# A hybrid encoder block on one core: the mixer in two calls, half of the tokens retrieved between them, and the rows of one sparse tile gathered earlier

## The chip, the cores and the metric

The kernel runs on one core of one Trainium2 chip. The metric is the device time of one execution in microseconds (us); the time of the kernel before is the median of three runs. The trace comes from one further execution that was profiled; its span (first to last instruction) and its own device time stand side by side in the table below.

## The reference

One layer on x of 1024 tokens x 1024 features, all float32:

```
proj = x @ w_in
A    = gated DeltaNet(4 heads x 128: causal conv of 4 on q, k, v; chunked delta rule; gated RMS norm)
B    = sliding-window attention(8 query heads x 64, 2 kv heads, window 128, learned sinks)
x1   = LayerNorm(alpha * x + concat(A, B) @ w_out)
per head of 8 (product keys): q1, q2 = halves of x1 @ wq;  s1 = q1 @ keys1^T, s2 = q2 @ keys2^T   (128 keys each)
       top 16 of s1, top 16 of s2, top 16 of their 256 sums -> ids = 128 * key1 + key2, gate = softmax
ffn  = sum over the 128 picks of a token: gate * gelu(x1 . u[id]) * v[id]      (16384 experts, u and v of 1024 features)
out  = LayerNorm(alpha * x1 + ffn)
```

The recurrence of A runs over the tokens in order. What token t retrieves needs x1 of token t alone.

## The kernel before

All sizes are in tiles of 128 tokens (`NT` = 8). The function `build` (L2042) calls the stages one after the other; `stage_semaphores` ends each with a barrier of all engines, so that no stage overlaps the next.

`project` (L118) computes the projections and writes them to DRAM. It is not touched.

`mix_tokens` (L365) runs over the eight tiles in order. Inside a tile the triangular solve is a chain of seven levels (`LV` = 6 and a last one): PE multiplies (L629, L632), DVE masks (L919), adds (L926, L934) and hands back to PE. Between the steps of the chain DVE does pieces of the next tile (`ahead`, L830), and PE does pieces of the output projection of the tile before (`project_out`, L520). After the levels DVE updates the recurrent state (L957), normalizes the two halves of the mix (L963 to L977), and finishes the layer norm of the tile before (`layer_norm` L882, `normalize` L897). POOL applies scale and shift to that row block `h1`, and SP stores it (L494), which also paces SP's loads of x (L461). In the first tile DVE splits the eight 512 KB pieces of `w_out` into a high and a low part (`split_wout`, L904), and PE has no output projection there. SP's loads are L458, L461 and L483.

`split_x1` (L1005) loads x1 (L1023), transposes it and splits it into high and low parts for PE.

`retrieve` (L1049) does the eight heads for all eight token tiles at once: queries on PE, scores, then the selection on DVE (L1279 is its first operation of a head, L1339 its last, L1353 a part of the tail), the turning of positions into keys on POOL and ACT. On PE it also computes the first 12 of the blocks of `hidden` (matmul of u against x1 for the dense tokens) that a later stage would otherwise do.

`index_picks` (L1420) computes the row numbers `id_u`, `id_v` and transposes the picks of the dense tiles.

From here the tokens are in two halves. Tiles 0 to 3 (`NS` = 4) are **sparse**: for each of a tile's 128 picks, POOL gathers 128 rows of u (one for each token, 128x1024, one indirect DMA of 512 KB), and DVE takes the dot product with x1 (one instruction and a read of its accumulator; rings of `U_RING` = 4 buffers). For v, POOL gathers 128 rows by token (`V_RING` = 6 buffers), and PE sums them with weights: a **V step** is four gathered blocks and 8 matmuls of 128x32 by 128x512 (`weigh_rows`, L1804), 32 steps a tile. Tiles 4 to 7 are **dense**: all 16384 experts are computed for them with a gate that is zero where an expert was not picked.

`build_gates` (L1468) makes that gate for the dense tiles: 32 steps of 16 tokens. In each, DVE builds one-hot rows `g_two` (L1549, 16 instructions) and `g_one` (L1555, 16), PE multiplies them (L1511, 16 matmuls), ACT copies the result, and SP stores 4 MB after every fourth step (`s_G<-g_tile`). Beside it POOL gathers the U rows of sparse tile 0 (L1566), DVE dots them (L1540, four a step), and PE computes 8 more hidden blocks (L1523 to L1525, six matmuls of 128x512 in each step), with DVE splitting u (L1533).

`experts` (L1617) runs over 64 groups of 256 experts. A group loads its u, v and gate (L1706 is the gate), computes hidden (L1778 to L1780, left out for the first `SHORT` = 10 groups, whose hidden blocks exist by then), the gating, and the values (L1799 to L1801), which DVE adds up (L1946). Beside this run the sparse tiles: `PHASE` says at which groups tile s begins. Between two of them DVE takes the dots of tile s+1 (L1742 gathers, L1955 dots; 128 rows spread over the phase's length less one group) and PE weighs the V rows of tile s (L1751 gathers, L1813 matmuls). The last lines norm and store the output.

What sets the order is each engine's program text, with counted semaphores between engines, and the two tables that `spread` (L1607) makes from `PHASE`:

```
PHASE = (0, 18, 36, 54, 64)
for s in range(NS - 1):   spread(PHASE[s], PHASE[s + 1] - 1.0, P, U_SLOTS)        # U rows of tile s + 1
for s in range(NS):       spread(PHASE[s] + 0.5, PHASE[s + 1] - 0.1, 32, V_SLOTS) # V steps of tile s
```

## Time and profile before

| what | value |
|---|---|
| device time, median of 3 runs | 3643.05 us |
| lowest and highest | 3635.28 and 3651.44 us |
| the profiled execution, its own device time | 3627.19 us |
| its span | 3625.5 us |
| mean granted clock of TensorE | 0.893 of full |
| busy: PE / DVE / ACT / POOL | 2872.9 / 2381.2 / 931.5 / 1537.2 us |
| DMA over the span | 829.68 MB, mean 229 GB/s |

The stages, by the first instruction of each: project 0 to 302.66, mixer to 791.79, split to 812.86, retrieval to 1234.20, numbering to 1242.66, gates to 1675.16, experts to the end; the third phase's end (group 54) lies at 3222.38. A stage's length counts in full, since a barrier stands between two of them. A busy time is the time in which an engine executed something; a share of DMA is the mean busy share of the 16 DMA engines.

### The profile page before, as it was taken

To read this page: it belongs to the slowest core of one execution; us is meant where nothing else is said; L and a number is where in the kernel's file an instruction comes from. 1 tells how busy PE (TensorE), PEld (TensorE's weight loads), DVE (VectorE), ACT (ScalarE), POOL (GpSimd) and SP (SyncE) were. 2 spreads that over 40 slices of the span, in tenths; PEclk is the share of its full clock that TensorE was granted. 3 is DMA by queue.
4 is the path that set the end of the run, shared out by engine and by line. 5 is a ranking of instruction groups with operands and counts; after the bars stand their busy time and mean duration, and the time that the engine had idled before them with its cause. 6 is when DMAs were issued, how large, how long until landed. Compare 5 with 4: busy or idle time off the path is not lost.

```text
span 3625.5 us, 40035 instructions
## 1 busy us (share of the span) xinstructions
PE 2872.9 (79%) x14408; PEld 2219.2 (61%) x14408; DVE 2381.2 (66%) x5368; ACT 931.5 (26%) x1295; POOL 1537.2 (42%) x1196
## 2 busy tenths in 40 slices
PE   7996899969776355553667989999998998898886
PEld 6896788857665254452344666666676666665554
DVE  4403666645999899994667767777676766653335
ACT  4312222223333233331111222222222222222111
POOL 0000011113776543334565655666655565633333
PEclk9987999989888677776788999999999999999998
DMA  4312121112110377777999999999999999977774
GB/s 136 116 47 83 59 61 61 42 65 74 44 44 25 107 253 240 272 263 282 345 368 370 375 344 334 377 340 367 353 332 354 351 358 350 345 264 263 265 260 166
DMA packets 367789, 829.68 MB, mean 229 GB/s; under 512 B 158048, under 2 KB 180704, under 8 KB 366592
## 3 DMA queue, kind: packets, MB, share of 16 engines
q0 software_dynamic: 150864, 548.60, 41.1%
q1 hardware_dynamic: 216752, 278.84, 23.2%
q8 instruction: 100, 1.64, 0.2%
q14 instruction: 73, 0.60, 0.0%
HBM read 768.49 MB, written 58.85 MB: 228 GB/s over the span
## 4 chain that ended last, share of the span: by engine, by line
DMA 23%; PE 12%; DVE 9%; POOL 6%; issue 3%; ACT 1%; SPq 0%; POOLq 0%; DVEq 0%; ACTq 0%
DMA e_vr<-in_v 10%; DMA hold<-in_v,id_v 6%; DMA e_u_row<-in_u,id_u 5%; POOL hold L1751 4%; PE psum L1813 4%; DVE e_u_row L1955 3%; DVE e_y L1946 2%; PE psum L1799 2%; PE psum L1800 2%; PE psum L1801 1%; POOL e_u_row L1742 1%; DMA e_g<-s_G 1%; PE psum L1778 1%; DVE e_vl L1917 1%; PE psum L1780 1%
## 5 line engine op out<-in xcount | busy, mean ns | idle before, releaser
L1751 POOL DMA_INDIRECT hold<-in_v,id_v x512 | 565.0, 1104 | 421.1 <-PE psum L1813 285.2
L1742 POOL DMA_INDIRECT e_u_row<-in_u,id_u x384 | 467.1, 1217 | 473.4 <-DVE hidden_s L1955 376.1
L1955 DVE CUSTOM_DVE_ANT_0 e_u_row<-e_u_row,hold 128x1024 f32<-128x1024 f32 x384 | 466.9, 1222 | 101.9 <-DMA e_u_row<-in_u,id_u 101.7
L1799 PE MATMUL psum<-e_vh,e_ah 128*128 128x512 f32 x1024 | 432.0, 422 | 112.7 <-DVE e_y L1946 104.5
L1800 PE MATMUL psum<-e_vl,e_ah 128*128 128x512 f32 x1024 | 418.9, 409 | 0.0
L1946 DVE TENSOR_TENSOR e_y<-e_y,psum 128x512 f32<-128x512 f32 x504 | 328.5, 680 | 134.1 <-PE psum L1801 133.9
L1801 PE MATMUL psum<-e_vh,e_al 128*128 128x512 f32 x1024 | 415.8, 406 | 0.0
L1813 PE MATMUL psum<-hold,e_column 128*32 128x512 f32 x2048 | 276.3, 661 | 170.5 <-DMA hold<-in_v,id_v 170.5
L1799 PEld LDWEIGHTS psum<-e_vh,e_ah 128*128 128x128 f32 x1024 | 204.3, 200 | 237.9 <-DVE e_y L1946 121.2
L1778 PE MATMUL psum<-x1d_hi,e_uh 128*128 128x512 f32 x864 | 343.1, 397 | 0.0
L1511 PE MATMUL psum<-g_one,g_two 128*128 128x128 f32 x1024 | 187.9, 368 | 191.3 <-issue 175.5
L1779 PE MATMUL psum<-x1d_lo,e_uh 128*128 128x512 f32 x864 | 337.4, 390 | 0.0
L1780 PE MATMUL psum<-x1d_hi,e_ul 128*128 128x512 f32 x864 | 336.5, 389 | 0.0
L1511 PEld LDWEIGHTS psum<-g_one,g_two 128*128 128x128 f32 x1024 | 182.7, 281 | 204.2 <-issue 204.2
L1929 DVE TENSOR_TENSOR e_a<-e_a,e_g 128x512 f32<-128x512 f32 x108 | 74.5, 690 | 311.8 <-ACT e_a L1858 157.9
L1566 POOL DMA_INDIRECT hold<-in_u,id_u x128 | 166.4, 1300 | 248.3 <-DVE hidden_s L1540 219.4
L1813 PEld LDWEIGHTS psum<-hold,e_column 128*32 128x32 f32 x2048 | 61.1, 116 | 307.1 <-issue 301.6
L1858 ACT ACTIVATE e_a<-psum 128x512 f32<-128x512 f32 x108 | 64.1, 593 | 678.9 <-PE psum L1780 678.9
L1801 PEld LDWEIGHTS psum<-e_vh,e_al 128*128 128x128 f32 x1024 | 203.9, 199 | 46.5
L1917 DVE TENSOR_TENSOR e_vl<-e_vr,e_vh 128x1024 fp32r<-128x1024 f32 x128 | 156.2, 1220 | 112.5 <-ACT e_vh L1847 112.5
L1800 PEld LDWEIGHTS psum<-e_vl,e_ah 128*128 128x128 f32 x1024 | 204.8, 200 | 40.9
L1847 ACT ACTIVATE e_vh<-e_vr 128x1024 fp32r<-128x1024 f32 x128 | 135.3, 1057 | 358.7 <-DMA e_vr<-in_v 352.3
(313 smaller groups left out, 5639.3 us busy)
## 6 DMA issues: line engine op xcount, KB each, us to landing
e_vr<-in_v SPq DMA_DIRECT2D x128, 512.0 KB, 6.6
e_ur<-in_uT SPq DMA_DIRECT2D x108, 512.0 KB, 6.9
s_G<-g_tile SPq DMA_DIRECT2D x8, 4096.0 KB, 13.8
e_g<-s_G SPq DMA_DIRECT2D x128, 256.0 KB, 13.1
p_wr<-in_w_ch SPq DMA_DIRECT2D x17, 512.0 KB, 3.8
s_ch<-p_out POOLq DMA_DIRECT2D x16, 512.0 KB, 3.8
m_ch<-s_ch SPq DMA_DIRECT2D x8, 1024.0 KB, 5.9
r_w<-in_wq SPq DMA_DIRECT2D x16, 512.0 KB, 4.1
```

What stands on the lines that cost most here:

```text
L1511: last = nc.tensor.matmul(psum[:, n // 4, (n % 4) * NK:(n % 4 + 1) * NK], one2[s][:, n, :], one1[s][:, n, :], start=True, stop=True)
L1742: pool.indirect_dma_start(out=u_ring[n % U_RING][:], out_offset=None, in_=io["u"], in_offset=bass.IndirectOffsetOnAxis(ap=id_u[:, s, k:k + ...
L1751: pool.indirect_dma_start(out=v_ring[m % V_RING], out_offset=None, in_=io["v"], in_offset=bass.IndirectOffsetOnAxis(ap=id_v[:, t:t + 1], a ...
L1778: nc.tensor.matmul(psum[:, j, :], uh[j][:, k, :], x1d[0][:, k, :], start=(k == 0), stop=False)
L1779: nc.tensor.matmul(psum[:, j, :], uh[j][:, k, :], x1d[1][:, k, :], start=False, stop=False)
L1780: last = nc.tensor.matmul(psum[:, j, :], ul[j][:, k, :], x1d[0][:, k, :], start=False, stop=(k == KC - 1))
L1799: nc.tensor.matmul(acc, ah[s][j][:, r], vh[s][j][:, c], start=(j == 0), stop=False)
L1800: nc.tensor.matmul(acc, ah[s][j][:, r], vl[s][j][:, c], start=False, stop=False)
L1801: last = nc.tensor.matmul(acc, al[s][j][:, r], vh[s][j][:, c], start=False, stop=(j == 1))
L1813: last = nc.tensor.matmul(psum[32 * j:32 * j + 32, 6 + c, :], column[:, n % Z_RING, j, 31 - i:63 - i], v_ring[(4 * n + j) % V_RING][:, c * ...
L1946: add = nc.vector.tensor_tensor(y[:, t, c], y[:, t, c], psum[:, 2 + q % 4, :], ALU.add)
L1955: nc.vector.tensor_tensor_reduce(row, row, xs[:, s, :], 1.0, 0.0, ALU.mult, ALU.add, hs[:, s, k:k + 1]).then_inc(dotted, 1)
```

## The change

The mixer is called twice, for tiles 0 to 3 and for tiles 4 to 7; the state and the small per-tile factors live outside it, its loops are written out, the input `xt` and `mixT` have one buffer instead of two, and the scores' buffer `sc` half its size. Each call loads and splits `w_out`. Between the calls `split_x1`, `retrieve` and a new `number_rows` (the part of `index_picks` that computes `id_u`, `id_v`, `gate_s`) run for the 512 sparse tokens. After the second call `split_x1`, `retrieve` and a new `turn_picks` (the other part) run for the 512 dense tokens. The second retrieval computes 16 hidden blocks, two a head, all of them split on DVE or ACT and none on POOL; the first computes none. No hidden block is left in `build_gates`, so that 16 are ready for `experts` instead of 20.

The second mixer call gathers the 128 U rows of sparse tile 0 on POOL and takes the dots on DVE; two of its four ring buffers are the landing buffers of `w_out`, so the first gather waits for the last split. `build_gates` gathers the V rows of sparse tile 0 and weighs them, one V step after each step's one-hot matmuls, and builds `g_one` with one instruction a step. `experts` has sparse tiles 1 to 3 left for V and begins with the U rows of tile 1.

The core of the diff:

```diff
-TAIL = 4
-AHEAD_R = PH + TAIL
-AHEAD_G = TD // TG
+AHEAD = 2 * PH
-PHASE = (0, 18, 36, 54, 64)
-AHEAD = AHEAD_R + AHEAD_G
+PHASE = (0, 11, 32, 53, 64)
...
+            ring = [sb(f"m_row{n}", [P, D]) for n in range(U_RING)]
+            wout_raw = ring[:2]
...
+                def dot_rows(count):
+
+                    if dots:
+                        for k in islice(row_numbers, count):
+                            if k == 0:
+                                dve.wait_ge(x0_in, 16)
+                            dve.wait_ge(row_in[k % U_RING], 16 * (k // U_RING + 1))
+                            row = ring[k % U_RING][:]
+                            nc.vector.tensor_tensor_reduce(row, row, x0[:], 1.0, 0.0, ALU.mult, ALU.add,
+                                                           hs[:, 0, k:k + 1]).then_inc(dotted, 1)
...
                         if n < LV - 1:
+                            if before:
+                                dot_rows(2)
                             dve.wait_ge(lt, c * (LV - 1) + n + 1)
                             nc.vector.tensor_tensor(tu[:, 0], tu[:, 0], bank(2), ALU.add).then_inc(la, 1)
...
                         if not before and n:
                             split_wout(n - 1)
+                        if before:
+                            dot_rows(1)
...
                     if after:
                         begin_inverse(c + 1)
+                    if before:
+                        dot_rows(4)
...
                     if not before:
                         for k in range(LV, KC):
                             split_wout(k)
+                        dot_rows(20)
+                    dot_rows(4)
...
                     last.then_inc(S["og"], 1)
+                    dot_rows(4)
...
                     if before:
                         normalize(c - 1)
+                    dot_rows(4)
...
+                def gather_rows(c):
+                    for k in range(c * P // N, (c + 1) * P // N):
+                        if k >= U_RING:
+                            pool.wait_ge(dotted, k - U_RING + 1)
+                        else:
+                            pool.wait_ge(wout_lo, KC)
+                        pool.indirect_dma_start(out=ring[k % U_RING][:], out_offset=None, in_=io["u"],
...
+                for c in range(N):
+                    if dots:
+                        gather_rows(c)
+                    if c:
+                        scale_shift(c - 1)
+                scale_shift(N - 1)
...
+def number_rows(nc, sem, cst, psum, key1, key2, gate, id_u, id_v, gate_s):
+                nc.vector.scalar_tensor_tensor(idf[:], key1[:], float(NK), key2[:], ALU.mult, ALU.add).then_inc(numbered, 1)
...
+def turn_picks(nc, sem, scr, cst, psum, key1, key2, gate, xs, pickT):
...
+                def weigh_rows(n):
...
-                        nc.tensor.matmul(out, uh[:, k, :], x1d[0][:, k, :], start=(k == 0), stop=False)
-                        nc.tensor.matmul(out, uh[:, k, :], x1d[1][:, k, :], start=False, stop=False)
-                        last = nc.tensor.matmul(out, ul[:, k, :], x1d[0][:, k, :], start=False, stop=(k == KC - 1))
+                    weigh_rows(q)
...
-                    for n in range(R):
-                        t = q * R + n
-                        last = nc.vector.tensor_scalar(one1[s][:, n, :], iota, pickT[:, 0, t:t + 1], None, ALU.is_equal)
-                    last.then_inc(hot1[s], 1)
-                    if q % PER == 0:
-                        split_u(q // PER)
-                    dot_rows(U_STEP * q + U_STEP // 2, U_STEP * (q + 1))
+                    nc.vector.tensor_tensor(one1[s][:], iota.unsqueeze(1).broadcast_to([P, R, NK]),
+                                            pickT[:, 0, q * R:(q + 1) * R].unsqueeze(2).broadcast_to([P, R, NK]),
+                                            ALU.is_equal).then_inc(hot1[s], 1)
...
-        for s in range(NS):
+        for s in range(1, NS):
             for at, ns in spread(PHASE[s] + 0.5, PHASE[s + 1] - 0.1, 32, V_SLOTS).items():
-                steps[at] = [32 * s + n for n in ns]
+                steps[at] = [32 * (s - 1) + n for n in ns]
```

**DVE in the levels of the mixer.** A tile's levels on DVE, before: m_tu is the solve's buffer, m_xs the masked product, m_dm, m_qd and m_aq belong to the next tile.

```order
L917 REGISTER_ALU
L919 TENSOR_TENSOR m_xs<-psum,cst 128x512
L846 ISA
L847 TENSOR_TENSOR m_qd<-m_ch,m_eg 128x512
L925 REGISTER_ALU
L926 TENSOR_TENSOR m_tu<-m_tu,psum 128x512
L934 TENSOR_TENSOR m_tu<-m_tu,psum 128x512
L851 TENSOR_TENSOR m_aq<-psum,m_dm 128x512
L917 REGISTER_ALU
L919 TENSOR_TENSOR m_xs<-psum,cst 128x512
L925 REGISTER_ALU
```

The same place in the second call after the change (L926 is now the dot and the read of its accumulator, L948 and L956 are the former L926 and L934; a name that ends in _4 is a buffer of the second call):

```order
L939 TENSOR_TENSOR m_xs<-psum,cst 128x512
L926 ISA m_row_4,hidden_s<-m_row_4,m_x_4 128x1024
L926 ISA hidden_s 128x1
L926 ISA m_row_4,hidden_s<-m_row_4,m_x_4 128x1024
L926 ISA hidden_s 128x1
L948 TENSOR_TENSOR m_tu<-m_tu,psum 128x512
L956 TENSOR_TENSOR m_tu<-m_tu,psum 128x512
L852 TENSOR_TENSOR m_dm<-psum,m_e_4 128x512
L926 ISA m_row_4,hidden_s<-m_row_4,m_x_4 128x1024
L926 ISA hidden_s 128x1
L939 TENSOR_TENSOR m_xs<-psum,cst 128x512
L855 TENSOR_TENSOR m_qd_4<-m_ch_4,m_eg 128x512
```

Three dots of 128x1024 have come into each level, two of them ahead of the addition for which PE waits.

**POOL in the second mixer call.** After the change (m_h is the row block h1 of the layer norm, m_row the ring):

```order
L1033 DMA m_row_4<-in_u,id_u 128x1024 x64
L1039 TENSOR_TENSOR m_h_4<-m_h_4,m_lng 128x1024
L1041 TENSOR_TENSOR m_h_4<-m_h_4,m_lnb 128x1024
L1033 DMA m_row_4<-in_u,id_u 128x1024 x32
L1039 TENSOR_TENSOR m_h_4<-m_h_4,m_lng 128x1024
L1041 TENSOR_TENSOR m_h_4<-m_h_4,m_lnb 128x1024
```

64 gathers stand ahead of the first scale and shift, and 32 ahead of each of the next two. Before, POOL had only the pairs of scale and shift in this stage.

**PE in the gate building.** Two steps before:

```order
L1511 MATMUL psum<-g_one,g_two 128x128 x16
L1523 MATMUL psum<-x1d_hi,g_uh 128x512
L1524 MATMUL psum<-x1d_lo,g_uh 128x512
L1525 MATMUL psum<-x1d_hi,g_ul 128x512
L1523 MATMUL psum<-x1d_hi,g_uh 128x512
L1524 MATMUL psum<-x1d_lo,g_uh 128x512
L1525 MATMUL psum<-x1d_hi,g_ul 128x512
L1511 MATMUL psum<-g_one,g_two 128x128 x16
```

And its beginning after the change (L1537 turns the activated dots of tile 0, L1545 is the former L1511):

```order
L1537 MATMUL psum<-cst,hidden_s 128x128
L1545 MATMUL psum<-g_one,g_two 128x128 x16
L1530 MATMUL psum<-hold,g_column 32x512 x8
L1545 MATMUL psum<-g_one,g_two 128x128 x16
L1530 MATMUL psum<-hold,g_column 32x512 x8
```

Six matmuls of 128x512 a step have left, and eight of a gathered block against a 32-column weight have come.

## Rows read from the trace of the kernel before

**Rows 1.** Windows: length, busy us of PE, PEld, DVE, ACT, POOL; PEclk, DMA, GB/s

```profile
302.66:791.79 489.13, 417.47 (x2756) 365.78 (x2756) 280.79 (x504) 123.42 (x268) 37.78 (x16) 0.92 0.18 56
791.79:812.86 21.07, 10.06 (x64) 8.41 (x64) 9.80 (x8) 8.20 (x8) 0.00 (x0) 0.81 0.50 199
812.86:1234.20 421.34, 293.07 (x1312) 240.72 (x1312) 367.50 (x1639) 151.13 (x129) 261.10 (x109) 0.84 0.13 46
...
1242.66:1675.16 432.50, 232.47 (x1216) 213.90 (x1216) 389.22 (x1288) 144.16 (x144) 166.38 (x128) 0.75 0.71 248
1675.16:3222.38 1547.22, 1323.65 (x6170) 938.56 (x6171) 1071.50 (x1618) 336.27 (x505) 908.15 (x774) 0.92 0.97 353
3222.38:3590.00 367.62, 307.45 (x1502) 201.93 (x1501) 135.55 (x176) 71.32 (x116) 124.05 (x123) 0.95 0.74 248
```

**Rows 2.** Windows, same columns: four tiles in the middle of the mixer

```profile
455.00:665.00 210.00, 199.04 (x1376) 174.29 (x1375) 133.32 (x240) 54.63 (x125) 18.12 (x9) 0.98 0.17 52
```

**Rows 3.** Timeline of SP in the mixer: start, us, engine, line, transfer [idle before]

```profile
302.66 0.33 SPq L474 DMA_DIRECT2D m_sinks<-in_sinks  x1
...
458.47 0.37 SPq L494 DMA_DIRECT2D s_x<-m_h  x1
...
511.57 0.36 SPq L494 DMA_DIRECT2D s_x<-m_h  x1
...
721.29 0.35 SPq L494 DMA_DIRECT2D s_x<-m_h  x1
...
768.93 18.60 SPq L494 DMA_DIRECT2D s_x<-m_h  x2
791.79 3.75 SPq L1023 DMA_DIRECT2D t_x<-s_x  x8
```

**Rows 4.** Timeline of DVE: the first operation behind the mixer's preparation

```profile
314.82 0.69 DVE L835 COPY m_gB<-m_rows 128x1024 f32<-128x1024 f32 x1
```

**Rows 5.** Waits of DVE, 455 to 665: total us, times, longest

```profile
DVE m_tu L926 <- PE psum L629: 46.9, 20, 3.6
...
DVE m_on L977 <- PE psum L668: 4.8, 4, 1.9
```

**Rows 6.** Timeline of DVE in the gates: the first dot

```profile
1248.90 1.23 DVE L1540 CUSTOM_DVE_ANT_0 hold<-hold 128x1024 f32<-128x1024 f32 x1 [1.82 <-DMA hold<-in_u,id_u]
```

**Rows 7.** Timeline of POOL in the gates: the first and the fifth gather

```profile
1243.44 1.02 POOL L1566 DMA_INDIRECT hold<-in_u,id_u  x1 [10.49 <-POOLq L115]
...
1250.40 1.83 POOL L1566 DMA_INDIRECT hold<-in_u,id_u  x1 [2.13 <-DVE hidden_s L1540]
```

**Rows 8.** U gathers of the gates, L1566, all 128

```profile
DMA to landing us min/median/max: 4.2/5.2/15.2
```

**Rows 9.** The same line while a 4 MB store is under way, 1349 to 1364

```profile
DMA to landing us min/median/max: 10.9/12.9/14.3
```

**Rows 10.** DVE's last operation of a head, L1339: ns min/median/max, first to last start

```profile
L1339 DVE TENSOR_TENSOR gate<-r_ex,r_gsum x8: 291/3252/3257, 894.2 to 1213.1; 128x128 f32<-128x128 f32 x8
```

**Rows 11.** Lines of DVE in the gates: busy us, mean ns | idle before

```profile
L1549 DVE TENSOR_SCALAR g_two<-cst,hold 128x128 f32<-128x128 f32 x512 | 134.2, 348 | 5.9 <-PEq L115 5.9
```

**Rows 12.** A comparison of 128x2048 on DVE, L1353

```profile
L1353 DVE TENSOR_TENSOR hold<-r_pf,cst x1: 2276/2276/2276, 1216.3 to 1216.3; 128x2048 f32<-128x2048 f32 x1
```

**Rows 13.** Page, costliest groups, the gates' U gathers: busy, mean ns | idle before

```profile
L1566 POOL DMA_INDIRECT hold<-in_u,id_u x128 | 166.4, 1300 | 248.3 <-DVE hidden_s L1540 219.4
```

**Rows 14.** U gathers of the experts, L1742, all 384

```profile
DMA to landing us min/median/max: 4.3/8.2/10.6
```

**Rows 15.** Timeline of PE in the last phase: two V steps

```profile
3244.61 1.92 PE L1813 MATMUL psum<-hold,e_column 128*32 128x512 f32 x16
...
3253.64 1.92 PE L1813 MATMUL psum<-hold,e_column 128*32 128x512 f32 x16 [1.42 <-DMA hold<-in_v,id_v]
```

**Rows 16.** V gathers of the last phase, L1751, 3240 to 3590: count, then landing

```profile
L1751 POOL DMA_INDIRECT hold<-in_v,id_v x122: 932/941/1980, 3246.8 to 3573.4; - x122
...
DMA to landing us min/median/max: 4.1/6.0/10.9
```

More of the change, by code:

```diff
@@ L1015, in part @@
         def part(t, which):
-            x1, first = (x1s, 0) if t < NS else (x1d, NS)
-            return x1[which][:, :, (t - first) * P:(t - first + 1) * P]
+            return x1[which][:, :, t * P:(t + 1) * P]
         with nc.Block() as block:
@@ L1036, in _ @@
             def _(act):
-                for t in range(NT):
+                for t in range(NT // 2):
                     act.wait_ge(tr[t % 2], t // 2 + 1)
@@ L1042, in _ @@
             def _(dve):
-                for t in range(NT):
+                for t in range(NT // 2):
                     dve.wait_ge(hi[t % 2], t // 2 + 1)
@@ L1117, in store_hidden @@
                     sp.dma_start(scr["hidden"][b], act_out[b % 2][:]).then_inc(h_out[b % 2], 16)
-                def head(h):
+                for h in range(PH):
                     for s in range(2):
@@ L1477, in build_gates @@
         PER = TG // R
-        U_STEP = P // STEPS
-        xs = hold[:, 0:NS, :]
-        ring = [hold[:, 6 + n, :] for n in range(U_RING)]
+        x0 = hold[:, 0, :]
+        ring = [hold[:, NS + n, :] for n in range(V_RING)]
         one1 = [sb(f"g_one{s}", [P, R, NK]) for s in range(2)]
@@ L2086, in build @@
[L2086 to L2087 removed]
+        with ExitStack() as mixer:
+            small = {n: sb(mixer, f"m_{n}", [P, NT, GH])
+                     for n in ("lnbeta", "g", "gam", "nkey", "kdl", "kdec", "nbeg", "decay", "beta")}
+            rows = sb(mixer, "m_rows", [P, NT, 2, GH])
+            state = sb(mixer, "m_state", [P, GH, P])
+            with stage_semaphores(nc) as sem:
+                mix_tokens(nc, sem, io, scr, ba, cst, psum, small, rows, state, 0)
+            with ExitStack() as sparse:
+                x1s = [sb(sparse, f"x1s_{n}", [P, KC, TS], F32R) for n in ("hi", "lo")]
+                key1, key2, gate = picks(sparse, "early")
+                with stage_semaphores(nc) as sem:
+                    split_x1(nc, sem, scr, cst, psum, x1s, 0)
+                with stage_semaphores(nc) as sem:
+                    retrieve(nc, sem, io, scr, cst, psum, x1s, key1, key2, gate, False)
+                with stage_semaphores(nc) as sem:
+                    number_rows(nc, sem, cst, psum, key1, key2, gate, id_u, id_v, gate_s)
+            with stage_semaphores(nc, "_late") as sem:
+                mix_tokens(nc, sem, io, scr, ba, cst, psum, small, rows, state, NS, dots=(id_u, hs))
```

781 lines of the change are left out of this document (382 added, 399 removed).

## The prediction

> **What bounds the kernel now.** I read the windows by stage first, because a barrier stands between stages and each one's length counts in full. In [rows 1] the reader sees six different limits. The mixer (489.13 us) has PE busy for 417 us and DVE for 281: it is a chain that passes between the two, and in its middle PE is busy 199.04 of 210 us [rows 2]. The retrieval (421.34 us) has DVE busy for 367.5. The gates (432.50 us) have DVE busy for 389.22, and the experts' first 54 groups (1547.22 us, 28.65 a group) have DMA at 0.97 with 353 GB/s and PE busy for 1323.65, 24.5 a group. The last ten groups (367.62 us, 36.8 a group) have DMA at 0.74, PE at 307 and DVE at 136. Nothing is full there, and the timeline of PE shows why: V steps start at 3244.61 and 3253.64, 9.0 us apart, the second after a wait for gathered rows [rows 15]. 122 gathers from 3246.8 to 3573.4 are 10.7 us for four [rows 16], so 32 steps take 32 x 10.7 = 342 us of that phase. The change takes work from the two DMA- and DVE-bound stages and gives it to the mixer, where DVE shows 8 idle microseconds in 20. The question is whether those are free.
>
> **The mixer in two calls: +62.** The stores of the row blocks date the tiles [rows 3]: the first block is stored 155.8 after the stage's start, the next 53.1 later, the last but one 47.6 after the one before it, the last 18.3 later (they are the pair of 18.60), and 4.6 after it the next stage begins. A call of four tiles is 155.8 + 53.1 + 47.6 + 18.3 + 4.6 = 279.4. The second call has no preparation of the small factors; DVE's first tile work starts 12.2 after the stage's start [rows 4], of which some 4.7 for the loads stays, so 7.5 go. 2 x 279.4 - 7.5 - 489.1 = +62. The repeated w_out split is inside the 155.8.
>
> **The 128 dots: +139.** A dot takes 1.23 us on DVE [rows 6]. In the first late tile 24 stand in a row behind the last split, and a ring of four feeds them. The first gather starts only then: in the gates the first gather started at 1243.44 and the first dot at 1248.90, 5.5 later [rows 6, 7]. A buffer's cycle is the issue's gap 0.3, 5.2 to landing [rows 8], 1.23 for the dot and a little for the hand-over, 7.0 in all, so 1.75 a row: 24 x 1.75 = 42. Eight more at about 1.5 are 12, of which DVE's wait for PE at L977 (1.2 a tile [rows 5]) covers 1.9 with its neighbours. Nothing else of the chain can pass DVE meanwhile. Sum 5.5 + 42 + 12 - 2 = 58. In each of the other three tiles 32 dots are 39.2 us. Two in each of five levels stand where DVE waited for PE anyway, 46.9 us in four tiles, and the 4.8 at L977 also [rows 5]: 12.9 a tile are covered. The rest, 26.3, is on the chain, and with one short wait for a ring emptied while POOL does a scale and shift (18.12 us for nine operations [rows 2], two a tile) it is 27, in three tiles 81. 58 + 81 = +139. PE's fill work hides behind this, not the other way round. Bounds: 104 dots' excess entirely covered, +58; nothing covered and each at the ring's pace, at 1.83 + 0.3 a row [rows 7], 128 x 2.13 + 5.5 = +278.
>
> **Retrieval +53, split and numbering +12.5.** L1339 ends DVE's work of a head: 894.2 to 1213.1 for eight, 45.6 a head [rows 10]. The first head ended 81.3 after the start [rows 1, 10], so 36 went before DVE's first selection, and 21 after the last. With half the tokens a head costs 23.3 (half of the selection, small operations whole). Call one, without hidden blocks: 24 to start, 8 x 23.3, 11 of tail = 222. Call two has two splits of u a head, 2.4 us of DVE, and loads twice as many: 32 + 8 x 26.1 + 11 = 252. Together 474 against 421.3. The loads of x1 and the barriers come twice: +7 for the split, +5.5 for the numbering (8.46 before).
>
> **The gates: -42.** DVE falls far below the stage: g_two costs 134.2 for 32 steps [rows 11], and one comparison of 128x2048 took 2.28 us [rows 12], so 4.2 + 2.3 = 6.5 a step. What ends last is the V chain. Its step is 9.0 in [rows 15] and 10.7 as a mean of the phase [rows 16]. To the 9.0 to 9.4 that two steps there show I add 0.8 for slower issue beside DVE's comparisons (1300 ns [rows 13] against a median of 941 [rows 16], twice in a chain) and 0.5 for a lower clock, since PEclk is 0.75 here [rows 1]: 10.6, times 32 = 339. Seven stores of 4 MB meet the gathers; while one is under way landing takes 12.9 instead of 5.2 [rows 8, 9]. Not all of 7.7 shows, I take 6.3: 44. With 7 to start the stage is 390 against 432.5. Bounds: no gain (0), and 32 x 9.0 + 12 = 300 (-132).
>
> Here a row and a rule differ in size. POOL's gather took 1.83 us right behind a dot, 1.02 at the start of the stage [rows 7], and 1300 ns is the mean of all. The Trainium skill (SBUF — State Buffer, "SBUF: two separate sides") says that GpSimd cannot write the descriptors of its transfers while a VectorE instruction of certain kinds holds the port pair that they share. By that rule every gather beside DVE would take the 1.83: two on a V step's chain make 1.8 us instead of 0.8, 32 more for the gates, and a row of the burst takes 2.13 instead of 1.75, 9 more. The sum would be +145 instead of +104.5. I take the measured mean of 1300 ns, in which both kinds are mixed; the rule's size lies within my range.
>
> **The experts: -120.** 128 gathers of V rows leave, 67 MB. Groups 0 to 10: U rows of tile 1 are 12.8 a group instead of 7.5, no V rows, no hidden in the first eight. DVE was busy 19.8 a group [rows 1]; 5.3 dots at 1.3 more make 26.7. The ring of four gives one row in (8.2 + 1.23 + 0.3) / 4 = 2.4 us at the experts' landing time [rows 14], less when V gathers don't compete: 31 a group at most. I take 29.5: 325 for eleven. Groups 11 to 52, 42 of them: 6.4 U rows and 1.5 V steps a group are 9.0 MB, which at 353 GB/s [rows 1] is 25.5, close to PE's 24.0 to 24.5. I take 26.3: 1105. The last eleven groups hold the same 32 steps and no U rows, 32 x 10.7 plus the lead-in: the same 368 [rows 1, 16]. The tail of 35.5 stays. 325 + 1105 + 368 + 35.5 = 1833 against 1950, and with four more hidden loads and matmuls less an early start of the V steps I round to -120. Bounds: -75 (27.3 a group) and -178 (PE alone at 24.5, short groups at 28).
>
> **Sum.** 62 + 139 + 53 + 12.5 - 42 - 120 = +104.5. On the span of 3625.5 this is 3730, on the profiled execution's own 3627.19 about 3732. The median shown, 3643.05, lies 16 above that execution, so the median is 3732 + 16 = 3748; I say **3747 us**.
>
> **Rivals.**
> 1. *TensorE's clock falls in the places that DVE now holds up* (chance 0.14). The mixer's granted clock is 0.98 where PE is busy 95% [rows 2], and 0.75 in the gates, where it is busy 54% [rows 1]. A late tile of 80 us with 50 of PE work would, at the lower level (1.2 GHz instead of 2.4), need up to 100: 3 x 20 = 60, and a V step's 1.92 [rows 15] would become 3.84, part of 32 x 1.9. About +85: 3830. Against it: hidden blocks and fill remain. The Trainium skill (TensorE: Matmul & The Clock Gate, "HAM oscillation") holds that an engine which keeps waiting between bursts is throttled again; by it this rival would be the rule.
> 2. *The costs come as worked out, but the chains relax* (0.10): the gates at 341 (-92, V steps of 9.4 and stores hidden) and the experts at -172. Net +2.5: 3646, no change.
> 3. *The experts turn out DMA-bound throughout, and lose what DMA loses* (0.10), the other side. 65 MB at 353 GB/s [rows 1] are 184 us; if groups 11 to 52 take 24.7, the first eleven 25, and the last phase's V steps run at 9.4, near the 9.0 of [rows 15], for 32 x 1.3 = 42 less, the stage is 1676, -274, net -50: 3593. It decides once the experts save more than 224 us, that is all other terms together. Against it: PE's 24.5 a group leaves no room, and the last phase was slow with DMA at 0.74 already.
>
> **How the numbers follow.** The forecast, 3700 to 3790, has 0.66. The range takes in the second rival and half of the first: 3640 to 3830. 0.5% (18 us) is about what a measurement of this kernel can tell from no change. Faster: rival 3 and a bit of rival 2, 0.11. Same: the rest of rival 2, 0.09. Slower: the forecast and rival 1, 0.80.
>
> **What would show it.** The first late tile should hold a block of 24 dots on DVE of 45 to 50 us with PE idle, its tiles 1 to 3 should take near 80 us between stores, and DVE's wait at the level's first addition should have gone. The two calls of the mixer should sum to about 690, the retrievals to 474, the gates should be near 390 with PE's V matmuls waiting for POOL's rows and DVE under 60% busy, groups 11 to 52 near 26 us with DMA still over 0.95. It is wrong if the mixer calls sum to under 620 (the dots hid), if the gates are over 430 or under 330, or if PEclk in the second mixer call is under 0.85.

## The result and the profile after

| | before | after |
|---|---|---|
| device time, median | 3642.5 us (4 runs) | 3766.57 us (4 runs) |
| lowest to highest | 3635.28 to 3651.44 | 3760.72 to 3789.43 |
| ratio, 95% interval | | 1.035 (1.030 to 1.040) |
| profiled execution, own time and span | 3627.19, 3625.5 | 3760.72, 3759.1 |
| TensorE's granted clock | 0.893 | 0.875 |
| busy PE / DVE / ACT / POOL | 2872.9 / 2381.2 / 931.5 / 1537.2 | 2868.1 / 2388.5 / 951.4 / 1576.6 |

The change costs 3.5%, with the forecast of 3747 us 20 us below the median and inside the range. The busy time of each engine moved by under 3%. What changed is where the work stands, and what waits for it there. The windows by stage of the kernel after (window, length, busy us of PE, PEld, DVE, ACT, POOL, then PEclk, DMA share, GB/s) answer to [rows 1]:

```profile
301.55:574.63 273.08, 214.81 (x1380) 188.11 (x1380) 146.57 (x264) 68.01 (x144) 18.84 (x8) 0.87 0.20 60
574.63:588.35 13.72, 5.81 (x32) 5.00 (x32) 4.90 (x4) 4.10 (x4) 0.00 (x0) 0.72 0.41 153
588.35:809.60 221.25, 118.49 (x512) 98.13 (x512) 182.42 (x862) 70.12 (x89) 150.43 (x106) 0.75 0.14 43
...
812.86:1043.82 230.96, 118.07 (x688) 103.55 (x688) 152.97 (x251) 37.68 (x72) 82.74 (x66) 0.70 0.62 202
1043.82:1129.17 85.35, 55.41 (x344) 47.53 (x344) 74.44 (x127) 13.86 (x31) 46.64 (x34) 0.82 0.65 211
1129.17:1209.39 80.22, 48.31 (x296) 40.48 (x296) 68.50 (x116) 10.55 (x27) 44.07 (x34) 0.82 0.69 223
1209.39:1239.56 30.17, 13.41 (x48) 10.43 (x48) 7.07 (x13) 0.29 (x1) 4.68 (x2) 0.73 0.15 52
1239.56:1253.92 14.36, 5.80 (x32) 4.99 (x32) 4.90 (x4) 4.10 (x4) 0.00 (x0) 0.71 0.40 147
1253.92:1515.22 261.30, 201.58 (x896) 165.52 (x896) 197.57 (x878) 114.20 (x134) 158.89 (x106) 0.89 0.26 85
1515.22:1524.30 9.08, 3.00 (x12) 2.15 (x12) 0.36 (x1) 2.60 (x5) 0.00 (x0) 0.50 0.61 231
1524.30:1914.49 390.19, 233.56 (x1537) 146.54 (x1537) 206.57 (x548) 121.25 (x163) 129.91 (x128) 0.78 0.71 259
1914.49:2250.27 335.78, 176.04 (x609) 137.24 (x610) 258.52 (x410) 51.74 (x63) 167.08 (x138) 0.74 0.89 300
2250.27:3351.51 1101.24, 1062.45 (x5049) 784.38 (x5049) 808.22 (x1194) 280.83 (x408) 609.30 (x508) 0.99 0.95 342
3351.51:3723.60 372.09, 326.03 (x1598) 219.77 (x1597) 148.38 (x192) 77.15 (x124) 124.20 (x123) 0.96 0.75 252
3723.60:3759.10 35.50, 12.29 (x47) 9.02 (x45) 28.36 (x41) 7.68 (x10) 20.64 (x8) 0.69 0.30 118
```

In order: first mixer call, split, retrieval of the sparse half (the numbering of 3.3 us is left out), the second mixer call in four pieces that end at its stores and its last barrier, split, retrieval of the dense half, turning of the picks, gates, experts in groups 0 to 10, 11 to 52, 53 to 63, and the tail. As a balance of the spans:

| stage | before | forecast of the difference | measured after | difference |
|---|---|---|---|---|
| mixer, 1 or 2 calls | 489.1 | +201 | 273.1 + 426.7 | +210.7 |
| split of x1 | 21.1 | +7 | 13.7 + 14.4 | +7.0 |
| retrieval | 421.3 | +53 | 221.3 + 261.3 | +61.3 |
| numbering, turning | 8.5 | +5.5 | 3.3 + 9.1 | +3.9 |
| gates | 432.5 | -42 | 390.2 | -42.3 |
| experts and tail | 1950.3 | -120 | 1844.6 | -105.7 |
| projection | 302.7 | 0 | 301.6 | -1.1 |
| span | 3625.5 | +104.5 | 3759.1 | +133.6 |

The spans differ by 133.6 us and the medians by 124, since the profiled execution of the kernel before lies 15 us below its median and that of the kernel after 6. A stage also differs from one execution to the next: the experts' code of the kernel after, from their first load to the end, took 1844.6, 1862.8, 1829.3, 1867.5, 1864.8 and 1865.0 us in the profiled executions of that kernel and of runs 1 to 5 below. Fifteen us more or less in that stage are therefore no finding.

The loss is in the second mixer call. The waits of DVE (total us, times, longest), over that whole call:

```profile
DVE m_row L926 <- DMA m_row<-in_u,id_u: 43.5, 43, 5.6
DVE m_h L895 <- PE psum L527: 13.6, 1, 13.6
DVE m_tu L948 <- PE psum L630: 13.3, 10, 4.3
DVE m_sc L874 <- PE psum L533: 9.2, 4, 2.7
```

DVE waits 43.5 us for gathered rows, where [rows 5] have no such wait; 25.7 us of it lie in the first late tile, up to 962. Its wait for PE at the level's first addition (now L948) is 13.3 us. The page's rows of what POOL and DVE do there and in the gates answer to [rows 13] and [rows 11]:

```profile
L1033 POOL DMA_INDIRECT m_row<-in_u,id_u x128 | 156.6, 1224 | 226.6 <-DVE hidden_s L926 122.8
L1580 POOL DMA_INDIRECT hold<-in_v,id_v x128 | 129.9, 1015 | 255.4 <-PE psum L1530 215.9
L1562 DVE TENSOR_SCALAR g_two<-cst,pickT 128x128 f32<-128x128 f32 x512 | 134.4, 351 | 156.2 <-PE psum L1545 156.2
...
L1530 PE MATMUL psum<-hold,g_column 128*32 128x512 f32 x512 | 103.6, 952 | 142.0 <-DMA hold<-in_v,id_v 142.0
```

The gates' DVE now waits 156 us for PE, and the gates' V matmuls wait 142 us for rows: the bound of that stage moved from DVE to the chain of gather, landing and V step.

### The profile page after: what moved, and what is told of

Same layout as the page of the kernel before. It is cut to its first block, busy times and chain, and to the rows that moved or that the text cites. A ratio compares the mean times of both kernels' runs of the same rounds, so it can differ in the third digit from the quotient of the medians.

```text
span 3759.1 us, 39825 instructions
## 1 busy us (share of the span) xinstructions
PE 2868.1 (76%) x14408; PEld 2200.5 (59%) x14408; DVE 2388.5 (64%) x4994; ACT 951.4 (25%) x1389; POOL 1576.6 (42%) x1299
## 4 chain that ended last, share of the span: by engine, by line
PE 23%; DMA 14%; DVE 8%; issue 2%; POOL 2%; ACT 1%; POOLq 0%; SPq 0%; DVEq 0%; ACTq 0%
DMA e_vr<-in_v 5%; DMA hold<-in_v,id_v 4%; PE psum L1827 4%; DMA e_u_row<-in_u,id_u 4%; PE psum L1813 4%; PE psum L1814 3%; PE psum L1815 3%; PE psum L1792 3%; PE psum L1793 3%; PE psum L1794 3%; DVE e_u_row L1969 3%; DVE e_y L1960 2%; DMA e_g<-s_G 1%; DVE e_vl L1931 1%; POOL hold L1765 1%
## 5 line engine op out<-in xcount | busy, mean ns | idle before, releaser
L1792 PE MATMUL psum<-x1d_hi,e_uh 128*128 128x512 f32 x896 | 355.4, 397 | 0.0
L1793 PE MATMUL psum<-x1d_lo,e_uh 128*128 128x512 f32 x896 | 350.4, 391 | 0.0
L1794 PE MATMUL psum<-x1d_hi,e_ul 128*128 128x512 f32 x896 | 349.3, 390 | 0.0
L1033 POOL DMA_INDIRECT m_row<-in_u,id_u x128 | 156.6, 1224 | 226.6 <-DVE hidden_s L926 122.8
L1562 DVE TENSOR_SCALAR g_two<-cst,pickT 128x128 f32<-128x128 f32 x512 | 134.4, 351 | 156.2 <-PE psum L1545 156.2
L1827 PE MATMUL psum<-hold,e_column 128*32 128x512 f32 x1536 | 192.2, 619 | 48.2 <-DMA hold<-in_v,id_v 48.0
L1530 PE MATMUL psum<-hold,g_column 128*32 128x512 f32 x512 | 103.6, 952 | 142.0 <-DMA hold<-in_v,id_v 142.0
L1792 PEld LDWEIGHTS psum<-x1d_hi,e_uh 128*128 128x128 f32 x896 | 168.5, 188 | 73.3 <-issue 38.5
```

The lines of the kernel that those rows point to most:

```text
L1033: pool.indirect_dma_start(out=ring[k % U_RING][:], out_offset=None, in_=io["u"], in_offset=bass.IndirectOffsetOnAxis(ap=id_u[:, 0, k:k + 1 ...
L1792: nc.tensor.matmul(psum[:, j, :], uh[j][:, k, :], x1d[0][:, k, :], start=(k == 0), stop=False)
L1793: nc.tensor.matmul(psum[:, j, :], uh[j][:, k, :], x1d[1][:, k, :], start=False, stop=False)
L1794: last = nc.tensor.matmul(psum[:, j, :], ul[j][:, k, :], x1d[0][:, k, :], start=False, stop=(k == KC - 1))
L1827: last = nc.tensor.matmul(psum[32 * j:32 * j + 32, 6 + c, :], column[:, n % Z_RING, j, 31 - i:63 - i], v_ring[(4 * n + j) % V_RING][:, c * ...
```

## The experiments

Every run below was compared with the kernel before on the same chip; "before" is the median there. These medians lie between 3632.62 and 3639.84 us, that of the result at 3642.5, so a difference of 10 us between a run and the kernel after is not told apart. Spans are of the profiled execution.

**1. The dots left out.**

```diff
-                row_numbers = iter(range(P))
+                row_numbers = iter(())
...
-                    if dots:
-                        gather_rows(c)
```

> The changed kernel with its second mixer call stripped of the 128 gathers and dots of sparse tile 0 (left out of the computation: hidden_s of tile 0 is set to zero). Theory (the dots sit on DVE's side of the chain): the second call falls from 426.7 us to that of the first call less its preparation, 273 - 7.5 = 266, so the kernel loses some 160 us, 3767 -> about 3607; gates and experts stay within 5 us. Rival (the second call is long because w_out is loaded again and its tiles start cold, the dots are mostly covered): the call stays above 340 us and the kernel above 3680.

Measured: 3608.49 us against 3635.19 before, ratio 0.991 (0.988 to 0.995). The second call, from its first load at 818.00 to the next stage's at 1081.66, took 263.7 us; the theory said 266. Windows of that call here and, below, of the kernel after:

```profile
818.00:1081.66 263.66, 214.00 (x1376) 187.20 (x1376) 143.99 (x249) 62.35 (x131) 18.88 (x8) 0.89 0.21 64
```

```profile
812.86:1239.56 426.70, 235.21 (x1376) 201.98 (x1376) 302.98 (x504) 62.38 (x131) 178.13 (x136) 0.75 0.61 197
```

DVE's busy time differs by 159.0 us, the call's length by 163.0. The dots are paid in full; what they fill of DVE's idle time comes back as waits for rows. Here the same view of waits as above, without dots:

```profile
DVE m_tu L949 <- PE psum L630: 44.9, 20, 4.3
...
DVE m_rms L997 <- ACT m_rms L773: 5.7, 3, 1.9
DVE m_sc L875 <- PE psum L533: 3.9, 4, 1.1
DVE m_on L1007 <- PE psum L669: 3.5, 4, 1.0
```

At the level's first addition (L949 here) 44.9 became 13.3, so 31.6 us were indeed covered, and at L997 and L1007 some more; and 43.5 us of waits for rows took their place. The wait for PE at L875 (L874 in the kernel after) grew, from 3.9 to 9.2 us; "The clock" below returns to it. This run also shows that the rest of the change, without the price of the dots, is 27 us faster than the kernel before. The two calls of the mixer by themselves cost 273.1 + 263.7 - 489.1 = 47.7 us.

**2. The first late tile's 32 dots left out.**

```diff
-                        dot_rows(20)
-                    dot_rows(4)
+                    if before:
+                        dot_rows(4)
...
-                    if dots:
-                        gather_rows(c)
+                    if dots and c:
+                        gather_rows(c - 1)
```

> The changed kernel without the 32 dots of the first late tile (96 rows gathered and dotted, all in the three tiles behind it, at the same places; the last 32 rows are left out of the computation). Theory (24 dots in a row, fed by a ring of four, stop the chain, and 8 more): the call is shorter by 58 to 75 us, the kernel near 3700. Rival (PE has work to do meanwhile, and the price is in the levels of tiles 1 to 3): under 30 us.

Measured: 3704.41 us, 62 below the kernel after. The second call took 363.4 us, 63.3 less. That is near the 58 of the forecast, but the stores of the row blocks date it better. The first one comes 163.9 us after the call's start here and 231.0 in the kernel after, so the first tile's dots cost 67 us. The stretches behind it are alike (84.3 and 79.6 us between stores, against 85.4 and 80.2), up to the last store; from there to the next stage it is 9.3 us here, in which no engine works, and 4.1 in the kernel after and in run 1. What brings these 5 us was not tried. Without them the other 96 dots cost 363.4 - 263.7 - 5.1 = 94.6 us, 31.5 a tile where the forecast had 27.

**3. All dots in the three later tiles.**

```diff
                         if before:
-                            dot_rows(1)
+                            dot_rows(2)
...
-                    for k in range(c * P // N, (c + 1) * P // N):
+                    for k in range(c * P // 3, (c + 1) * P // 3):
...
-                    if dots:
-                        gather_rows(c)
+                    if dots and c:
+                        gather_rows(c - 1)
```

> The changed kernel with the same 128 dots, but none in the first late tile and 43, 43 and 42 in the three behind it (two instead of one at each level's end, 6, 6, 5 and 4 outside the levels). Theory (what counts is the number of dots on the chain at 1.23 us each, and the burst also pays 1.75 us a row for its ring and 5.5 for its start): 11 more dots in each of three tiles cost 13.5 us each, 40, against 58 to 75 saved: the kernel is 20 to 35 us faster than the changed one, about 3740. Rival (the ring of four cannot feed 43 rows a tile): as slow as the changed kernel or slower, with waits for rows inside the levels.

Measured: 3776.58 us, 10 above the kernel after: the theory's 20 to 35 us of gain did not come. The second call took 429.4 us against 426.7. Two tiles of it (1010 to 1218) have this view of waits on DVE:

```profile
DVE m_row L926 <- DMA m_row<-in_u,id_u: 33.6, 26, 6.0
DVE m_sc L874 <- PE psum L533: 5.5, 2, 2.7
```

These are 33.6 us of waits for rows in two tiles, up to 6.0 each, where the kernel after has 11.0 in the same two. The rival was right that the rows are what is short, but this run has a cause of its own beside the ring. The first two tiles gather 42 and 43 rows and take 43 dots each, so the last dot of either tile needs a row whose gather stands behind the scale and shift of the tile before. It waits 5.9 us in the first (to 1011.37) and 6.0 in the second (to 1121.30). These 11.9 us could hide more than half of a gain of 20. Without them the call would be some 9 us shorter than in the kernel after, still short of the theory; the rest are shorter waits, up to 5.0 us, at dots that follow one another closely, as the ring of four gives them. I had treated the ring's pace as a matter of the burst alone.

**4. Only the dots ahead of a level's first addition.**

```diff
-                row_numbers = iter(range(P))
+                row_numbers = iter(range(30))
...
-                        if before:
-                            dot_rows(1)
```

> The changed kernel with only the 30 dots that stand ahead of the first addition of a level (two in each of five levels of the three later tiles of the second call); the other 98 rows are left out of the computation. Without any dot DVE waited there for PE, 22.4 us in two tiles, and the second call took 263.7 us. Theory (dots in a place where DVE waits are free up to the length of that wait): 12.3 us of dots a tile against 11.2 of wait, the call stays under 275 us and the kernel near 3615. Rival (a dot costs its 1.23 us wherever it stands, since its row or PE's next work comes later too): 30 x 1.25 = 37 more, the call about 301 us, the kernel 3646.

Measured: 3623.97 us against 3632.62. The call took 280.6 us, between the two: 17 above the call without dots, not 37. DVE's waits in two of its tiles:

```profile
DVE m_row L927 <- DMA m_row<-in_u,id_u: 12.0, 2, 6.6
DVE m_tu L949 <- PE psum L630: 4.9, 6, 1.4
```

These two, 12.0 us, are the only waits for a row in the whole call; the first of the three tiles has none. From the call's start to its first store, which holds that tile's ten dots, the call takes 142.7 us against 141.7 in run 1: ten dots, 12.3 us of work, cost 1.1. The next two tiles take 8.3 and 9.0 us more than in run 1, of which 5.4 and 6.6 are the waits for a row. So 12.0 of the 17 us are late rows, and some 5 are dots that were longer than their gap; over the call DVE is busy 34.2 us more, and its wait at L949 fell from 44.9 to 17.9. POOL's timeline of this run says where the row was:

```profile
956.89 2.36 POOL L1032 TENSOR_TENSOR m_h<-m_h,m_lng 128x1024 f32<-128x1024 f32 x1 [30.68 <-DVE m_h L909]
959.33 2.37 POOL L1034 TENSOR_TENSOR m_h<-m_h,m_lnb 128x1024 f32<-128x1024 f32 x1
961.84 0.98 POOL L1026 DMA_INDIRECT m_row<-in_u,id_u  x1
```

The first gather of the tile was issued at 961.84, behind the scale and shift of the tile before, and the dot that wanted it waited 5.40 us until 968.57. So a dot in a gap is nearly free, and here the first row of a tile is not, because of its place in POOL's queue. In the kernel after this particular wait does not occur: there a tile's last four dots stand behind the normalization, and the next tile's first dots come 12 us after its first gather (1056.12 and 1043.94) and wait for nothing.

**5. Nine buffers for the V rows of the gates.**

```diff
-        ring = [hold[:, NS + n, :] for n in range(V_RING)]
+        GR = 9
+        ring = [hold[:, NS + n, :] if n < V_RING else sb(f"g_row{n}", [P, D])[:] for n in range(GR)]
```

> The changed kernel with nine buffers instead of six for the V rows of the gate building (the experts keep six). Theory (the stage is a chain of gathers, landing and one V step, 11.8 us a step with PE waiting 142 us for rows): with a whole step's rows ahead the chain opens, and the stage goes from 390 us towards the bound of its bytes, 101 MB at 353 GB/s = 285, say 310: the kernel about 3690. Rival (ACT's evacuation or PE at the low clock bounds the step): the stage stays over 370.

Measured: 3683.55 us, 83 below the kernel after. The window of the stage:

```profile
1523.67:1819.00 295.33, 200.10 (x1537) 138.64 (x1537) 205.10 (x548) 123.84 (x163) 157.54 (x128) 0.83 0.91 342
```

295 us instead of 390, with DMA at 0.91 instead of 0.71. It is the chain that bound the stage. Opened, it stands near the 285 estimated from its bytes; that the bytes are the next bound was not tried. PE's wait for rows fell from 142.0 to 76.4 us. The stage is 95 us shorter and the medians 83 apart; the experts' 1865.0 us of this execution, against 1844.6, are of the size by which that stage differs anyway.

**6. One part of the change alone: `g_one` in one comparison.** (On the kernel before.)

```diff
-                    for n in range(R):
-                        t = q * R + n
-                        last = nc.vector.tensor_scalar(one1[s][:, n, :], iota, pickT[:, 0, t:t + 1], None, ALU.is_equal)
+                    nc.vector.tensor_tensor(one1[s][:], iota.unsqueeze(1).broadcast_to([P, R, NK]), ...
```

> The kernel before with one part of the change alone: g_one of a step in one comparison of 128x2048 (2.28 us) instead of sixteen (3.22). Theory (the gate building before is bound by DVE, 389 busy of 432): DVE loses 103.0 - 73 = 30 us and the stage the same, the kernel -30, 3635 -> about 3605. Rival (the U rows' ring or the gathers beside a comparison that reads two tensors hold it up): no gain, DVE's waits for rows grow from 25 by what the comparison saves.

Measured: 3615.51 us against 3639.84, ratio 0.994 (0.991 to 0.997). The stage is some 21 us shorter (busy DVE 389 to 358), and DVE's waits for rows grew from 25.3 to 34.3 us: the theory, less a third of the rival.

**7. Ten V buffers in the last phase.** (On the kernel before. The four U buffers are idle there.)

```diff
+        def v_slot(m):
+            return m % V_RING if m < LAST else (m - LAST) % (V_RING + U_RING)
```

> The kernel before with ten buffers instead of six for the V rows of the last phase alone (the four of the U rows are idle then). Theory (the last phase is bound by the chain of gather, landing and V step, 10.7 us a step): the phase goes from 367.6 us to PE's 307 with gaps, about 315, the kernel -50. Rival (the bound is the values' chain with DVE and the loads of u and v): within 10 us of the kernel before.

Measured: 3567.45 us against 3639.84, ratio 0.979 (0.974 to 0.984), more than expected. The last ten groups of this run:

```profile
3243.00:3537.00 294.00, 291.64 (x1501) 196.01 (x1500) 135.19 (x175) 71.40 (x116) 125.63 (x123) 1.00 0.88 310
```

294.0 us instead of 367.6, with PE busy for 291.6 of it at the full clock: the phase passed from a chain of latencies to PE. PE's busy time shrank by 16 us too, from 307.5 to 291.6, with its granted clock at 1.00 instead of 0.95 (307.5 x 0.95 = 292). That is why the gain passed the estimate, which had PE at 307.

**8. Runs 6 and 7 together**

> Both of the last two edits on the kernel before. They touch different stages with a barrier between them, so the gains add: -80, about 3555, faster than both kernels. Rival: the gains share a cause and do not add.

Measured: 3543.3 us against 3639.84, ratio 0.974 (0.968 to 0.980). The gains of 24 and 72 make 96, and 97 came. This version computes the whole result and beats the kernel before by 2.6% and the kernel after by 5.9%.

**9. Both rings on the kernel after**

> The changed kernel with nine buffers for the V rows in the gate building and ten for those of the last phase. Theory: the first gives the 83 us of its own run again, the second 350 -> 315 in the last phase: 3767 - 83 - 35 = 3649, level with the kernel before and behind the kernel before with its own two edits. Rival: the last phase does not move, 3684.

Measured: 3617.62 us against 3639.84, ratio 0.994 (0.991 to 0.997): the changed order with its two chains opened is slightly faster than the kernel before, and 74 us behind run 8. It was expected at 3649. The gates took the 296 us of run 5 again, and the experts and the tail 1810.4 us, 34 less than in the kernel after, as expected; the median came out 31 lower than the sum said, and the profiled execution, at 3632.21, only 17. The two rings together take 149 us off the kernel after.

**10. Experts without U rows.** (On the kernel after; `dots[at] = []`.)

> The changed kernel whose experts gather and dot no U rows (left out of the computation: the dots of sparse tiles 1 to 3 are zero); V rows and the dense part stay. It asks what bounds groups 11 to 52, 26.75 us each with PE busy 97% and DMA at 0.95. If DMA (3.3 MB of 9.0 a group gone): the groups fall to where PE stands, under 25.5. If PE (22.1 of hidden and values and 1.5 V steps of 1.92, 25.0, and short gaps): they stay over 26. In groups 0 to 10 (30.5 us each) the ring of four U rows and the dots are gone: the theory says they were the bound, so these fall to under 22 us each, 90 us less or more; the rival for these groups (the loads of v and the gate) says over 27.

Measured: 3586.22 us. Groups 0 to 10, and 11 to 52, by windows:

```profile
1905.49:2117.66 212.17, 155.93 (x602) 123.54 (x603) 113.36 (x154) 52.35 (x63) 5.43 (x6) 0.86 0.50 149
2117.66:3166.65 1048.99, 1048.99 (x5057) 778.88 (x5056) 536.33 (x682) 278.06 (x408) 261.35 (x256) 1.00 0.71 233
```

The 26.75 us a group and the 97% in the expectation, and the last phase's 350 in that of run 9, counted group 53 among the middle ones: counted rightly the kernel after has 1101.2 us for groups 11 to 52, 26.2 each, with PE busy 96%, and 372.1 for the last phase. The first eleven groups took 212.2 instead of 335.8 us without the U rows: these were their bound, the gain of some 123 more than the 90 expected. The next 42 took 1049.0 us, 25.0 each, with PE busy for every microsecond and DMA at 0.71. So 25.0 of the 26.2 are PE's own, and 1.2 is what the U rows add through DMA or DVE (0.3 of it as busy time of PE, 1062.45 against 1048.99 us in all). Neither theory was right alone: the groups fell under 25.5, but only by 1.2 us, and what they fell to is PE.

**11 and 12. A later last phase.** (On run 8, `PHASE = (0, 19, 38, 57, 64)` and `(0, 19, 38, 56, 64)`.)

> The kernel before with one comparison for g_one and ten V buffers in the last phase, and the phases moved to groups 0, 19, 38, 57. Now the last phase is bound by PE (busy 291.6 of 294 us, 28.2 a group) while DMA has 12% left, and the three before it are bound by DMA at 0.97. Theory: seven groups of the last phase cost PE 7 x 22.1 + 61 = 216 and DMA 85 MB / 353 = 242, so 245 instead of 294, and the phases before get 3 more groups' 7.9 MB, +22: about -25, 3518. Rival: the V chain (7.6 us a step wanted) is bound again even with ten buffers: no gain or a loss.

> As the run before, with phases at groups 0, 19, 38, 56. Theory: last phase 8 x 22.1 + 61 = 238 for PE and 250 for DMA, so 252 instead of 294, and +15 before it: -25, the same 3518. Rival: as in the run before, with a smaller loss.

Measured: 3555.42 and 3545.13 us, ratios 0.979 (0.976 to 0.982) and 0.974 (0.970 to 0.978) against 0.974 (0.968 to 0.980) of run 8. Neither gained. The last phase did what the theory said: in run 11 its seven groups took 245 us (3274.2 to 3519.5), where run 8 needs 294 for ten. But the groups ahead took 1615.2 us (from 1658.99) against 1563.9, 51 more instead of 22. The windows of run 8 and run 11:

```profile
1645.14:3209.05 1563.91, 1330.16 (x6170) 942.77 (x6171) 1071.35 (x1618) 336.34 (x505) 905.92 (x774) 0.92 0.97 349
```

```profile
1658.99:3274.21 1615.22, 1386.46 (x6458) 985.92 (x6459) 1109.30 (x1666) 355.03 (x529) 914.79 (x774) 0.93 0.95 343
```

DMA moved 349 GB/s in the one and 343 in the other, which at this length is some 28 us and accounts for the rest. Why the rate is lower was not tried, and it may not be the edit's doing: there is one profiled execution of each, and unchanged code of this stage differed by up to 38 us between executions of the changed kernel.

## Why the prediction was right, and where it was off

**The mixer in two calls, +62: 47.7.** The first call took 273.1, not 279.4, and the second without its dots 263.7, not 271.9: the first store of a call of four comes 151.1 us after its start (155.8 said). Which edit of the written-out loops brings that was not tried.

**The dots, +139: 163.** The mechanism holds: run 1 gives 163 for all. Both parts were put too low. The first tile's 32 dots cost 67, not 58 (the stores in run 2). Its 24 in a row are as forecast, a wait of 5.6 us and then 44.0 (898.63 to 942.60), with PE not busy at all; the eight behind them and what hangs on them cost 17 instead of 10.

The step that was mis-sized in the other three tiles is "with one short wait for a ring emptied while POOL does a scale and shift it is 27". The last two intervals between stores that hold 32 dots are 85.4 and 80.2 us, and 51.9 and 47.7 in run 1: 33.5 and 32.5 a tile. The covered part was not overrated, 31.6 us in three tiles at the additions alone. What was missing, for each of these tiles, is three things. The first is rows: 5.1 and 5.8 us of waits, counted at under 1. It isn't one wait but six and seven of at most 1.6 us, and nearly all fall on the dots that stand in fours behind the levels, which the ring of four cannot feed at DVE's pace (the 24 in a row came at 1.83 us each, against 1.22 for a dot):

```profile
1106.11 1.23 DVE L926 CUSTOM_DVE_ANT_0 m_row<-m_row,m_x 128x1024 f32<-128x1024 f32 x1 [1.40 <-DMA m_row<-in_u,id_u]
...
1108.96 1.23 DVE L926 CUSTOM_DVE_ANT_0 m_row<-m_row,m_x 128x1024 f32<-128x1024 f32 x1 [1.62 <-DMA m_row<-in_u,id_u]
```

The second is some 2.5 us of PE's lower clock, the third some 3 to 4 us of the port; both are below. No run took these three apart.

**Retrieval +53: 61.** A head of the sparse half takes 23.5 us (23.3 said; L1365 from 633.3 to 798.1), one of the dense half 27.1 (26.1 said; 1313.8 to 1503.7). DVE waits there 28.9 us for ACT's first parts of u, in four waits of up to 13.1, and these I had left out.

**The gates -42: -42.3.** The V step was said to take 10.6 us and the stores 44 for the stage; the steps are 11.8 us from first to last (1538.7 to 1905.4), the stores included. Run 5 shows the cause, not only the size.

**The experts -120: -105.7.** Groups 0 to 10: 325 said, 335.8 measured; run 10 confirms the U rows as the bound. Groups 11 to 52: 1105 said, 1101.2 measured. The size was right and the reason half: I had 26.3 from DMA's 25.5 and put PE at 24.0 to 24.5, while PE needs 25.0 by itself (run 10). The last phase: 368 said, 372.1 measured. The sum of the terms was 117, which I rounded to 120; of the 11 us that are left, the first eleven groups have 10.8. The whole difference of 14 is within what this stage differs by between executions.

**The clock.** I wrote that PEclk under 0.85 in the second call would make the prediction wrong. It was 0.75 there, and 0.82 in the middle tiles, so by that sign of mine the prediction is wrong; the sign was badly chosen, since the clock could fall without the price I tied to it. The first rival's cause happened, at a small part of its 85 us: PE was busy 235.2 us instead of 214.0 (run 1), 21 us more, of which about 7 show in the call's length. Ahead of each of the three later tiles PE sits idle while DVE takes dots, and then computes the scores (L533) for which DVE waits. The kernel after, then run 1:

```profile
1048.52 3.75 PE L533 MATMUL psum<-m_kw,m_ch 64*128 64x256 f32 x8 [8.69 <-DVE m_mixT_lo L1015]
```

```profile
956.01 1.96 PE L533 MATMUL psum<-m_kw,m_ch 64*128 64x256 f32 x8 [0.68 <-DVE m_mixT_lo L1016]
```

The granted clock around the first is 0.50, the lower level, and around the second 1.00:

```profile
1048.40:1054.30 5.90, 5.78 (x17) 4.60 (x18) 2.40 (x3) 0.00 (x0) 1.76 (x2) 0.50 0.89 328
```

DVE waits 2.74 us there instead of 0.95. Over the call its waits at L874 grew by 5.3 us and those at L939 (L940 in run 1), behind the next matmuls, from 0.7 to 2.3. The Trainium skill (TensorE: Matmul & The Clock Gate, "HAM oscillation") says that an engine that keeps waiting between bursts is throttled again; this trace agrees, 0.50 after an idle 8.69 us. In the last phase of the experts the clock counted once the chain was open (run 7).

**The port.** POOL's gathers in the second call took 1224 ns on average: the mean of 1300 from [rows 13] was a better price than 1.83 for each. A cost that I had not counted ran the other way: the scale and shift of POOL held DVE's dots, as this piece of DVE's timeline and then of POOL's shows, in the last tile but one:

```profile
1124.53 2.42 DVE L926 CUSTOM_DVE_ANT_0 m_row<-m_row,m_x 128x1024 f32<-128x1024 f32 x1 [0.86 <-DMA m_row<-in_u,id_u]
...
1126.87 3.35 DVE L926 CUSTOM_DVE_ANT_0 m_row<-m_row,m_x 128x1024 f32<-128x1024 f32 x1
...
1130.15 1.22 DVE L926 CUSTOM_DVE_ANT_0 m_row<-m_row,m_x 128x1024 f32<-128x1024 f32 x1
```

```profile
1123.36 2.50 POOL L1039 TENSOR_TENSOR m_h<-m_h,m_lng 128x1024 f32<-128x1024 f32 x1
1125.94 3.20 POOL L1041 TENSOR_TENSOR m_h<-m_h,m_lnb 128x1024 f32<-128x1024 f32 x1
1129.29 1.78 POOL L1033 DMA_INDIRECT m_row<-in_u,id_u  x1 [0.15 <-issue]
```

Dots of 1.22 us took 2.42 and 3.35 us while POOL's two operations of 128x1024 ran. The Trainium skill (SBUF — State Buffer, "SBUF: two separate sides") says that of two instructions that need the shared ports the one that starts first has them for its whole length and the other is blocked, and it names a VectorE instruction with two inputs in SBUF among those concerned. This trace agrees: the two dots end 1.1 us after the end of POOL's first and second operation (1126.95 after 1125.86, 1130.22 after 1129.14). They cost 3.3 us in this tile, and 2.9 and 4.1 in the others (1.95 and 3.35 from 1039.65, 3.18 and 3.35 from 1203.98).

**Sums that do not come out.** The experts' bound of -178 does not follow from its terms: 42 x 24.5 + 11 x 28 + 368 + 35.5 is 1740.5, which is -210. In the second rival 32 V steps of 9.4 and 7 to start are 308, not 341. The dots' lower bound speaks of 104 dots where 96 stand behind the first tile. None of them enters the forecast.

**How much of the closeness is luck.** The terms erred both ways: the mixer in two calls 14 us too high, the dots 24 too low, the retrieval 8 and the experts 14 too low. On the spans the forecast is 29 us short, on the medians 20.

## What to carry to other kernels

An idle share of an engine inside a dependent chain is not room for work: a gap of known length at a known wait is, if the data is there in time (run 4), and the rest is paid in full (run 1). A stage whose engines are all partly idle and whose gathers wait for the consumer is a matter of ring depth: three more buffers gave 83 us (run 5) and four idle ones 72 (run 7, on the kernel before), and both on the changed kernel 149 (run 9), more than the 124 us that the change lost. Before work is moved to feed an idle resource, look whether a deeper ring feeds it where it is.

## What the runs showed of the hardware

Where a chain opened, TensorE's clock rose too: with ten V buffers the granted clock of the last phase went from 0.95 to 1.00 and PE's busy time for the same work from 307 to 291.6 us. Where DVE held PE up, it fell: behind 8.69 us of idle time the clock was 0.50, and eight matmuls of 64x256 took 3.75 us instead of 1.96. Two of POOL's operations of 128x1024 stretched two of DVE's dots from 1.22 to 2.42 and 3.35 us. And a comparison of 128x2048 that reads two broadcast operands took 2.28 us where sixteen of 128x128 against a scalar took 3.22 in a row.
